# The norms' reciprocal as a rounded row and a rest row, spread over the partitions by one F32R product

## What is computed

```python
def rmsnorm(x, g, eps=RMS_EPS):
    xf = x.astype(jnp.float32)
    y = xf * lax.rsqrt(jnp.mean(xf * xf, axis=-1, keepdims=True) + eps)
    return (y * g.astype(jnp.float32)).astype(x.dtype)
...
    u = rmsnorm(h, p['norm_g'][l, 0]) * (1 + sc_m) + sh_m
    ...
    h = h + gt_m * rmsnorm(out, p['norm_g'][l, 1])
    u = rmsnorm(h, p['norm_g'][l, 2]) * (1 + sc_f) + sh_f
    ...
    h = h + gt_f * rmsnorm(out, p['norm_g'][l, 3])
```

## Time and profile before

| | |
|---|---|
| median of 3 runs | 3075.06 us (3073.81 to 3075.82) |
| the profiled execution, own time | 3085.03 us |
| its span, first to last instruction | 3082.9 us |
| mean granted TensorE clock | 0.974 |
| TensorE busy | 2923.2 us |
| DVE busy | 1547.8 us |
| GpSimd busy | 1326.7 us |
| ACT busy | 1050.5 us |

### The profile page before, as it was taken

One profiled execution on the slowest core, in us unless ns is written; L12 is line 12 of the kernel. 1 busy time (PEld: TensorE's weight loads), 2 busy tenths in 40 slices (PEclk: granted clock), 3 DMA queues, 4 the chain that ended last, 5 costly groups with the idle time before them and its releaser, 6 DMA issues.

```text
span 3082.9 us, 75512 instructions
## 1 busy us (share of the span) xinstructions
PE 2923.2 (95%) x30897; PEld 2764.4 (90%) x30897; DVE 1547.8 (50%) x2142; ACT 1050.5 (34%) x2026; POOL 1326.7 (43%) x949
## 2 busy tenths in 40 slices
PE   6999999998988899999999999989999999899998
PEld 6998999987977776899998799879999899799998
DVE  3436666127257775566612162466660345576612
ACT  4224333224443333433322443243332322433322
POOL 3443444433334444344444263434444344354443
PEclk9999999998999999999999899999999999899999
DMA  7554333543320003433354322353334443133332
GB/s 267 165 164 145 90 90 102 156 150 102 109 55 4 4 4 80 164 90 90 96 163 131 105 76 90 129 166 90 91 101 156 161 130 90 55 97 90 90 92 86
DMA packets 465627, 332.72 MB, mean 108 GB/s; under 512 B 19914, under 2 KB 435608, under 8 KB 465122
## 3 DMA queue, kind: packets, MB, share of 16 engines
q1 hardware_dynamic: 461400, 325.24, 34.2%
q10 hardware_dynamic: 4010, 4.22, 0.6%
HBM read 319.62 MB, written 10.20 MB: 107 GB/s over the span
## 4 chain that ended last, share of the span: by engine, by line
PE 56%; issue 5%; DVE 4%; POOL 3%; ACT 2%; DMA 1%; SPq 0%; POOLq 0%; DVEq 0%; ACTq 0%
PE banks L1615 32%; PE banks L1623 16%; POOL ct L893 2%; PE banks L2072 1%; PE banks L1918 1%; PE banks L1576 1%; DVE h L2554 1%; PE banks L1638 1%; PE banks L1709 0%; DVE proj L2498 0%; DMA s_state<-in_state_wkv_b_dram 0%; ACT conv L1064 0%; DVE rstd L2444 0%; POOL mmt L884 0%; DMA w_raw<-in_ffn_w_up_dram 0%
## 5 line engine op out<-in xcount | busy, mean ns | idle before, releaser
L765 POOL TENSOR_TENSOR w_lo<-w_raw,w_hi 128x1024 fp32r<-128x1024 f32 x395 | 1005.0, 2545 | 1120.5 <-ACT w_hi L965 1101.3
L1615 PE MATMUL banks<-u_hi,w_hi 128*128 128x260 f32 x4064 | 836.0, 287 | 13.4 <-ACT w_hi L965 9.4
L1615 PE MATMUL banks<-u_lo,w_hi 128*128 128x260 f32 x4064 | 826.8, 285 | 0.0
L1615 PEld LDWEIGHTS banks<-u_hi,w_hi 128*128 128x128 f32 x4064 | 628.7, 190 | 26.7 <-issue 14.6
L1615 PEld LDWEIGHTS banks<-u_lo,w_hi 128*128 128x128 f32 x4064 | 631.4, 190 | 1.8
L965 ACT ACTIVATE w_hi<-w_raw 128x1024 fp32r<-128x1024 f32 x402 | 424.5, 1057 | 455.3 <-PE banks L1623 302.9
L1623 PE MATMUL banks<-u_hi,w_lo 128*128 128x260 f32 x4064 | 528.6, 283 | 0.0
L1623 PEld LDWEIGHTS banks<-u_hi,w_lo 128*128 128x128 f32 x4064 | 502.5, 187 | 1.8
L1615 PE MATMUL banks<-hid_hi,w_hi 128*128 128x260 f32 x1664 | 336.5, 283 | 0.0
L1615 PE MATMUL banks<-hid_lo,w_hi 128*128 128x260 f32 x1664 | 335.2, 283 | 0.0
L2486 DVE TENSOR_TENSOR hid_lo<-prod,hid_hi 128x520 f32 x104 | 261.9, 2518 | 12.8
(11 more groups left out here) (462 smaller groups left out, 3954.4 us busy)
## 6 DMA issues: line engine op xcount, KB each, us to landing
w_raw<-in_ffn_w_up_dram SPq DMA_DIRECT2D x176, 512.0 KB, 3.6
ada_raw<-in_ada_w_dram SPq DMA_DIRECT2D x96, 512.0 KB, 4.7
w_raw<-in_ffn_w_down_dram SPq DMA_DIRECT2D x64, 448.0 KB, 3.5
w_raw<-in_sconv_w_in_dram SPq DMA_DIRECT2D x48, 512.0 KB, 5.3
ada_ahead<-in_ada_w_dram SPq DMA_DIRECT2D x36, 512.0 KB, 8.0
ada_ahead_down<-in_ada_w_dram SPq DMA_DIRECT2D x36, 512.0 KB, 6.5
w_raw<-in_ffn_w_down_dram SPq DMA_DIRECT2D x32, 512.0 KB, 3.8
ada_pro<-in_ada_w_dram SPq DMA_DIRECT2D x6, 2048.0 KB, 20.2
```

Source lines behind the costliest of these rows:

```text
L765: pool.tensor_tensor(w_lo[:, s, :, :], w_raw[:, s, :, :], w_hi[:, s, :, :].bitcast(F32), ALU.subtract).then_inc(lo_done, 1)
L1615: pe.matmul(tile_ps[slot][half][0:width, 0:HALF], w_hi[:, s, k, 0:width], x[:, k0 + k, half * HALF:(half + 1) * HALF], start=start and k = ...
```

## The change

`rstd` is no longer multiplied directly. Behind the reciprocal DVE now casts it to F32R (`rstd_rows`), and then forms `rstd_rows * rest_row + rstd` in place, again as F32R. `rest_row` is -1 on partition 32g+1 of each group and 0 elsewhere. So partition 32g keeps the rounded reciprocal and partition 32g+1 gets what rounding left out. The selector `row_sel` has ones in rows 32g and 32g+1 of column g, so that one F32R product adds the two rows into all 128 output partitions. `row_sel` and `rest_row` are made once, by three DVE instructions in the prologue. `rstd_rows` lies in the part of the `std` tile that the norms don't use.

```diff
@@ tiles
         rstd = sb("rstd", [P, T])
+        rstd_rows = at("rstd_rows", [P, NGW], F32R, std_at + 1056)
...
+        row_sel = sb("row_sel", [P, NG], F32R)
+        rest_row = sb("rest_row", [P, 1])
@@ TensorE
             def spread_rstd(norm):
 
                 pe.wait_ge(rstd_ready, norm + 1)
-                row = lambda g: ident[:, g * QUAD:g * QUAD + 1].to_broadcast([P, P])
-                pe.matmul(rstd_ps[1], row(NG - 1), rstd[:, NW:NGW], start=True, stop=True).then_inc(rstd_turned, 1)
+                row = lambda g: row_sel[:, g:g + 1].to_broadcast([P, P])
+                pe.matmul(rstd_ps[1], row(NG - 1), rstd_rows[:, NW:NGW], start=True, stop=True).then_inc(rstd_turned, 1)
                 for g in range(NG):
-                    mm = pe.matmul(rstd_ps[0][:, g * NW:(g + 1) * NW], row(g), rstd[:, 0:NW], start=True, stop=True)
+                    mm = pe.matmul(rstd_ps[0][:, g * NW:(g + 1) * NW], row(g), rstd_rows[:, 0:NW], start=True, stop=True)
                 mm.then_inc(rstd_turned, 1)
@@ DVE, prologue
             for s in (small_copied, tile_free[0], tile_free[1]):
                 dve.sem_inc(s, 1)
+            quad = ident[:, :].rearrange("p (g c) -> p g c", c=QUAD)
+            link(dve.tensor_tensor(row_sel[:, :], quad[:, :, 0], quad[:, :, 1], ALU.add))
+            link(dve.tensor_reduce(rest_row[:, :], quad[:, :, 1], AX.X, ALU.add))
+            link(dve.tensor_scalar(rest_row[:, :], rest_row[:, :], -1.0, None, ALU.mult))
@@ DVE, each norm
             def inverse_root(norm):
 
                 dve.wait_ge(std_done, norm + 1)
-                dve.reciprocal(rstd[:, 0:NGW], std[:, 0:NGW]).then_inc(rstd_ready, 1)
+                link(dve.reciprocal(rstd[:, 0:NGW], std[:, 0:NGW]))
+                link(dve.tensor_copy(rstd_rows[:, :], rstd[:, 0:NGW]))
+                dve.scalar_tensor_tensor(rstd_rows[:, :], rstd_rows[:, :].bitcast(F32), rest_row[:, 0:1], rstd[:, 0:NGW],
+                                         ALU.mult, ALU.add).then_inc(rstd_ready, 1)
```

## The result

The changed kernel is slower: 1.0028 times the kernel before, 95% interval 1.0016 to 1.0040 (medians of ten runs each 3086.52 and 3075.32 us; the single runs went from 3081.8 to 3091.4 and from 3073.8 to 3088.0). By the ratio that is 8.6 us, with 7 forecast; the two medians are 11.2 apart. The profiled execution took 3088.57 us with a span of 3086.8, only 4 above that of the kernel before, whose profiled execution (3085.03) was one of its longest; so the two traces are compared norm by norm and not by their spans.

The account below looks back on a forecast made before the run. TensorE was taken to bound the kernel (56% of the chain). Post norms +5.4, pre norms -0.4 and clock +2 sum to +7 us: 3082 against 3075.06, with 3079 to 3087 likeliest and a full range of 3074 to 3092.

Parts of the forecast that it names:

- the two mechanisms: GpSimd holding the new DVE instructions in post norms (+5.4 us), and TensorE's clock falling after longer idle (+2).
- The spread on TensorE: Each norm: five records instead of ten, 0.124 us apart, 0.77 us instead of 1.39; 0.62 saved, 1.09 at low clock.
- Rival (a): In the norms, the narrow F32R product lasts as long as its two f32 records: about +20 us, 3095; chance 0.2.
- DVE's two instructions alone: Each norm: cast 0.23 and scalar-tensor-tensor 0.35 us between reciprocal and product add 0.64 us with the start gaps.
- GpSimd's hold: Five post norms: cast and scalar-tensor-tensor end behind GpSimd's pieces one and two; TensorE starts 1.55 us behind the reciprocal.
- rival (b): Post norms: GpSimd doesn't hold the two new instructions, so not slower, 3073 to 3076 us; chance 0.25.
- What the use waits for in post norms: Five post norms: use waits for five low-clock records after TensorE's late start; +5.4 us in all.
- R + 3.1: Five post norms: R is the reciprocal's end; the spread row is used 3.1 us later, at the low clock.
- The pre norms: First hidden in the prologue, six at the high clock 0, one at the low clock -0.4 us.
- The clock behind: Behind pre norms: 2.2 us idle instead of 1.5 makes one or two more clock falls, 1.3 us each: +2 (0 to 4).
- Rival (c): The clock stays as it is while GpSimd does hold the new instructions: +3 to +5 us, 3079; no separate chance.

Follow-up runs that it names:

- The two runs that took the hold from these instructions in different ways: Changed kernel with GpSimd's post-norm weight pieces waiting for the F32R row: 1.0020; changed kernel with the reciprocal written to PSUM: 1.0014, both against the kernel before.
- fillers: Float32 identity matmuls before each wait for the row or reciprocal; against the kernel before: changed kernel with 8 or 11, 1.0007; kernel before with six, 0.9988 and 0.9987.
- the pair of runs above: Changed kernel with eight fillers and GpSimd starting after all additions to h, 3078.69 us; kernel before with six fillers, 3073.67 us; same job.
- TensorE's half alone: Changed kernel with the reciprocal rounded straight into the F32R row, without cast, scalar-tensor-tensor and rest row: 0.9983 of the kernel before, 3071.09 us.

## Why the prediction was right

The sign, the size (7 us forecast, 8.6 and 11.7 measured in two jobs, both in the range) and the two mechanisms held. Step by step:

**The spread on TensorE.** Spacing 0.123 us forecast from rows with other columns and types, 0.123 measured; 0.77 us from first start to last end, as forecast. At the low clock five records took 276.56 to 277.88, 1.32 us, with 1.41 forecast. Rival (a), a narrow F32R product without gain, is out. The Trainium skill ("TensorE: Matmul & The Clock Gate", Back-to-back issue gap) gives about 81 ns for each pair of weight load and matmul. Here that does not hold: the records with 128 columns of weights keep their 0.12 us in either type.

**DVE's two instructions alone.** 0.23 and 0.36, each starting 0.04 behind what it waits for: 0.67 us from the reciprocal's end (692.53) to the row (693.20) against 0.64.

**GpSimd's hold.** 0.69 and 0.72 us in the five post norms, against 0.65 and 0.75 forecast, and TensorE's start 1.53 to 1.54 us behind the reciprocal against 1.55. The two runs that took the hold from these instructions in different ways (1.0020 and 1.0014) were both below the changed kernel, if within overlapping intervals; the traces decide, and rival (b) is out. The Trainium skill has the rule ("GPSIMD Engine Reference", section 1, the row on SBUF interfaces: shared with VectorE, contention with DVE instructions in a 2-port mode or with two SBUF inputs), and the trace agrees: 0.69 us for a cast from SBUF beside GpSimd, 0.30 from PSUM.

**What the use waits for in post norms: the step that was wrong in kind.** I took the clock as low in all five norms and had the five records end last, with the use at R + 3.1; what GpSimd would do to L2546 behind the two new instructions I left out. It was held to the end of the fourth piece and was through at R + 2.83 whatever the clock. In the three norms at the low clock the records ended 0.03 us behind it (use at 2.97), in the two others half a microsecond ahead of it (2.86 and 2.87). With fillers the clock in these norms was kept, and the use stayed at 2.87. In these five the time from reciprocal to use grew by 4.6 us, where the forecast had 5.4; in the two with an early start of GpSimd it changed by +0.2 and -0.2 (0 forecast), and in the last, whose clock fell, it grew by 0.6 (0 or 0.7). Over all eight that is 5.3 us (16.9 to 22.1). That this is so near 5.4 is luck.

**The pre norms.** Forecast -0.4, from 0 in six norms and a gain in one. Measured +1.2 (11.8 to 13.0 us over seven): three gave 0.05 as forecast and the cold one gained 0.5, but in three that had been at the high clock the records fell to the low one, wholly or on the way, at 0.4 to 0.6 us each. I had put a fall only behind the norm, not into it.

**The clock behind.** +2 us (0 to 4) forecast; the runs with fillers give 3 to 5 for all that the longer idle time costs, the 1.2 us above among it. So the term was about right, at the upper end, as far as ratios across jobs can say. Rival (c), a clock that stays as it is, is out: three pre norms that had kept the clock now lost it, and fillers took 0.2% off the changed kernel.

Beside these the changed kernel has some 4 us more that I can't place (the pair of runs above, 5.0 us apart with 2.5 to either side, less than 1 of it in the norms). The forecast has no term for them.

## What to carry to other kernels

A detour to save passes on one engine has to be shorter than the passes while both lie on the same chain; here 0.64 us of DVE bought 0.62 us of TensorE, and the rest decided: what runs beside the new instructions, and for how long the waiting engine now idles. Before putting a DVE instruction with two SBUF inputs, or a fast cast, beside GpSimd work, count the piece boundaries it will have to wait for, and those of the held instruction that stands behind it; an operand in PSUM gets it past. Where TensorE waits a microsecond or two in each of many places, matmuls that write where the result will be overwritten anyway are a cheap trial, worth 0.12% in the kernel before. Where the low clock came all the same, they delayed the work behind them by 0.7 to 1 us.

## What was not expected of the hardware

- The length of a short idle time doesn't settle what becomes of the clock: after 1.60 us of idle the records of a post norm were at the high clock in the kernel before and at the low clock at the same place in TensorE's half alone (1.09 us for four); after 2.19 us of idle both occurred in one trace, 0.64 at 693.38 and 1.09 at 276.79.
- A hold by GpSimd hardly delays GpSimd: its four pieces took 2.83 us with three DVE instructions held against them and 2.79 with one. A held instruction ends behind the piece by 0.15 to 0.2 us less than its own time alone: by 0.08 us the cast (0.23 alone), by 0.15 the scalar-tensor-tensor (0.36), by 0.55 the 512-column addition (0.75). So part of it is done in the wait.
- Moving GpSimd's work behind the row moved the hold onto the next instruction with two SBUF inputs (1.30 us instead of 0.75), wherever the clock was kept: in three of seven post norms without fillers, in all seven with them. That gave back nearly half of the gain.
